# Two of the first loads of a decoder-block kernel move from SyncE's DMA queue to ScalarE's

## The reference

```python
h = rms_norm(x, norm_pre_mix[l])          # x: 512 x 1024
proj = h @ w_in[l]                        # w_in: 1024 x IN_COLS, in tiles of 128 columns
p_rwkv, p_nsa, p_swa, p_gate = _split(proj, (RWKV_COLS, NSA_COLS, SWA_COLS, GATE_COLS))
```

## Time and profile before

| what | us |
|---|---|
| median of 3 runs (lowest, highest) | 971.26 (971.24, 972.1) |
| the profiled execution, its own time | 971.14 |
| span in its trace (first to last instruction) | 969.3 |
| TensorE busy in the span | 949.5 (98%) |
| first matmul with a weight tile starts at | 14.74 |
| x3 issued at; last of it landed after | 2.89; 9.7 |
| w0 issued at; last of it landed after | 2.13; 9.1 |

### The profile page before, as it was taken

How to read it: one execution, slowest core, us unless ns; L and a number is a source line. 1 busy time by engine, 2 the same in 40 slices (tenths; PEclk the granted TensorE clock), 3 DMA queues, 4 the chain that set the end, 5 groups by cost and what they waited for, 6 DMA issues and landing times.

```text
span 969.3 us, 20667 instructions
## 1 busy us (share of the span) xinstructions
PE 949.5 (98%) x8504; PEld 767.3 (79%) x8504; DVE 703.2 (73%) x1170; ACT 422.5 (44%) x846; POOL 439.5 (45%) x473
## 2 busy tenths in 40 slices
PE   7999999999999999999999999999999999999997
PEld 5788777777777777776777888888999888888886
DVE  3799797565655966869777870489787774489987
ACT  4134341323313525546574454553444443345573
POOL 3367547335442865767665466445223225500000
PEclk9999999999999999999999999999999999999999
DMA  9344633212222648525336548043333433345452
GB/s 259 103 131 133 139 87 69 43 35 70 77 59 65 195 131 186 153 67 130 59 100 176 148 150 263 24 152 109 89 111 112 118 96 87 97 142 177 138 194 89
DMA packets 157365, 115.47 MB, mean 119 GB/s; under 512 B 21413, under 2 KB 139951, under 8 KB 157272
## 3 DMA queue, kind: packets, MB, share of 16 engines
q1 hardware_dynamic: 147820, 105.21, 37.8%
q10 hardware_dynamic: 9420, 8.95, 4.0%
q0 software_dynamic: 32, 0.00, 0.0%
HBM read 102.84 MB, written 11.30 MB: 118 GB/s over the span
## 4 chain that ended last, share of the span: by engine, by line
PE 83%; DVE 12%; issue 2%; ACT 1%; DMA 1%; POOL 0%; SPq 0%; DVEq 0%; ACTq 0%
PE ps L2424 32%; PE ps L2903 5%; PE ps L2902 5%; PE ps L2907 5%; PE ps L2544 3%; PE ps L2790 3%; PE ps L2963 2%; PE ps L2964 2%; PE ps L2965 2%; PE ps L2733 2%; PE ps L2940 2%; PE ps L2937 2%; PE ps L2936 2%; DVE XF L1517 2%; PE ps L2438 1%
## 5 line engine op out<-in xcount | busy, mean ns | idle before, releaser
L2424 PE MATMUL ps<-HHI,WHI 128*128 128x512 f32 x440 | 176.8, 402 | 0.7 <-DVE HLO L1549 0.7
L2424 PE MATMUL ps<-HLO,WHI 128*128 128x512 f32 x440 | 176.8, 402 | 0.0
L829 POOL TENSOR_TENSOR WLO<-WRAW,WHI 128x1024 fp32r<-128x1024 f32 (+1 forms) x51 | 103.2, 2026 | 102.1 <-ACT WHI L949 102.0
L930 POOL TENSOR_TENSOR WLO<-WRAW,WHI 128x512 fp32r<-128x512 f32 x50 | 72.5, 1457 | 118.6 <-ACT WHI L1317 117.2
L2424 PE MATMUL ps<-HHI,WLO 128*128 128x512 f32 x440 | 117.6, 397 | 0.0
L870 POOL TENSOR_TENSOR WLO<-WRAW,WHI 128x256 fp32r<-128x256 f32 x136 | 108.7, 802 | 14.4 <-ACT WHI L1166 7.0
L2424 PEld LDWEIGHTS ps<-HHI,WHI 128*128 128x128 f32 x440 | 82.6, 188 | 24.9 <-issue 7.5
L2424 PEld LDWEIGHTS ps<-HLO,WHI 128*128 128x128 f32 x440 | 82.6, 188 | 19.2 <-issue 1.6
L2424 PEld LDWEIGHTS ps<-HHI,WLO 128*128 128x128 f32 x440 | 80.7, 188 | 18.4 <-issue 1.4
L833 POOL CAST WHI<-WRAW 128x256 fp32r<-128x256 f32 (+1 forms) x93 | 46.7, 503 | 100.4 <-PE ps L2424 100.2
L2903 PE MATMUL ps<-HLO,WHI 128*128 128x512 f32 x200 | 77.9, 389 | 0.0
(11 more groups left out here) (512 smaller groups left out, 2316.1 us busy)
## 6 DMA issues: line engine op xcount, KB each, us to landing
WRAW<-in_w_in SPq DMA_DIRECT2D x47, 512.0 KB, 4.5
WRAW<-in_w_gate SPq DMA_DIRECT2D x22, 512.0 KB, 3.8
WRAW<-in_w_up SPq DMA_DIRECT2D x22, 512.0 KB, 3.8
WRAW<-in_w_down SPq DMA_DIRECT2D x19, 512.0 KB, 3.5
spilled<-SQ SPq DMA_DIRECT2D x24, 256.0 KB, 2.5
GATES<-spilled SPq DMA_DIRECT2D x6, 768.0 KB, 5.0
WRAW<-in_w_in SPq DMA_DIRECT2D x16, 256.0 KB, 3.5
WRAW<-in_w_branch SPq DMA_DIRECT2D x32, 128.0 KB, 2.9
```

The source lines that it names most:

```text
L829: return pool.tensor_tensor(lo[:, 0:chunks, :], WRAW[:, n % NRAW, 0:chunks, :], hi[:, 0:chunks, :].bitcast(F32), ALU.subtract)
L930: pool.tensor_tensor(lo, raw_half(item[1], item[2]), hi.bitcast(F32), ALU.subtract).then_inc(w_lo, 1)
L2424: last = pe.matmul(DB[g % 2][:, :], (wlo if which == "low" else whi)[:, c, :], lo if which == "x_low" else hi, start=a == 0, stop=a == 3 * ...
```

## The change

SP no longer issues x1 and w0. ScalarE issues both: x1 between `CONP` and the two `PRAW` loads, and w0 behind the `PRAW` loads, ahead of the square root. On SP's queue x3 moves up right behind x2, and w1 follows it. No semaphore, buffer or computation changes. The queues' orders become:

| queue | before | after |
|---|---|---|
| SP | x0, x1, x2, w0, x3, w1, `HOT`, sinks, `MASK`, w2, ... | x0, x2, x3, w1, `HOT`, sinks, `MASK`, w2, ... |
| ScalarE | `CONP`, `PRAW`, `PRAW` | `CONP`, x1, `PRAW`, `PRAW`, w0 |

```diff
--- before.py
+++ after.py
@@ -725,11 +725,9 @@
             def x_tile(t):
                 sp.dma_start(XTOK0[:, t, :], x[t * P:(t + 1) * P, :]).then_inc(x_in[t], 16)
 
-            for t in range(3):
+            for t in (0, 2, 3):
                 x_tile(t)
             for n in range(FF0):
-                if n == 1:
-                    x_tile(3)
                 if n == 2:
                     sp.dma_start(HOT[:, :], hot).then_inc(hot_in, 16)
                     sp.dma_start(SNK, bass.AP(sinks.tensor, 0, [[0, P], [1, NH]])).then_inc(hot_in, 16)
@@ -763,7 +761,7 @@
                             .then_inc(gates_in[(d - GS) % 2], 16)
                 if n >= NRAW:
                     sp.wait_ge(w_lo, n - NRAW + 1)
-                for part, cols, src in job_sources(n):
+                for part, cols, src in job_sources(n) if n else ():
                     sp.dma_start(raw_of(n)[part, :, cols], src).then_inc(w_loaded[n % NRAW], 16)
             sp.wait_ge(dense_done, OUT0)
             sp.dma_start(XTOK[:, :, :], x.rearrange("(t p) d -> p t d", p=P)).then_inc(xtok_in, 16)
@@ -934,8 +932,11 @@
         def _(act):
 
             act.dma_start(CONP[:, :], con[:, 0:NCONP]).then_inc(con_in, 16)
+            act.dma_start(XTOK0[:, 1, :], x[P:2 * P, :]).then_inc(x_in[1], 16)
             act.dma_start(PRAW[0:NPAR1, 0, :], par1).then_inc(par_in, 16)
             act.dma_start(PRAW[0:NPAR2, 1, :], par2).then_inc(par_in, 16)
+            for part, cols, src in job_sources(0):
+                act.dma_start(raw_of(0)[part, :, cols], src).then_inc(w_loaded[0], 16)
             act.wait_ge(eps_ok, 1)
             act.activation(MISC[:, 70:72], EPSC, ACT.Sqrt)
```

## The result

The changed kernel takes 978.71 us, the median of 4 runs (978.23 to 979.39), against 971.25 (970.96 to 972.1) before. The ratio is 1.0076, with a 95% interval from 1.0058 to 1.0093. It is 7.46 us slower. The forecast was 978.3.

The account below looks back on a forecast made before the run. TensorE, busy 98% of the span, was taken as the bound, so only its start could move: first weight-tile matmul 5.7 us later plus 1.3 us of slow clock, 7.0 us on 971.26, gives 978.3 us; range 971.7 to 981.0.

Parts of the forecast that it names:

- What bounds it: Whole kernel: TensorE is busy 98% of the span, so changed first loads move only the moment at which it gets going.
- Turns packet by packet: First loads: two queues share the DMA engines by packet count, not bytes; 72 packets on q1 against 67 on q10.
- my rival: First loads: queues share in lots of several packets, w0 lands with w1 at 14.4; +2.5 us, 973.8 us; chance 0.10.
- Landings: First loads: x1 and x2 land at about 9.3, x3 at about 10.8, w0 at 17.6 us, between 14.4 and 18.7.
- the few engines: w0's load: on engines holding most `PRAW` packets it waits 41 turns, 1.5 us beside x3 and 2.0 us beside w1.
- the slow partners: End of w0's load: its last 33 packets go beside `HOT`, the sinks and `MASK`, which take 2.6 us.
- From the landing to the first matmul: From w0's landing through `hi_part(0)`, `HHI` and `HLO`: 2.85 us, first weight-tile matmul at 20.45 instead of 14.74 us.
- What was taken as hidden: Start: issues, table load, parameters at about 12 and transposes ending at 15.7 us all come before w0 matters.
- x1's lateness: Start: x1 lands 1.5 us late from taking turns with x2; TensorE still ends its transposes well before w0's part.
- The clock: First matmuls after TensorE's 4.7 us idle: they run slow, costing 1.3 us, between 0 and 2.0.
- The not slower rival: Start: w0 lands by 11.9 us and TensorE's short waits for x go; -0.7 us, 970.6 us; chance 0.10.

Follow-up runs that it names:

- e3: Changed kernel with the 74-row parameter load cut into 64 and 10 rows: 974.17 us, ratio 1.0034 to the kernel before.
- e4: Changed kernel with `HOT`, sinks and `MASK` issued behind w2 instead of ahead of it: 975.08 us, ratio 1.0047 to the kernel before.
- e8: Changed kernel with both the 74-row parameter load cut in two and `HOT`, sinks and `MASK` behind w2: 973.34 us, ratio 1.0022 to the kernel before.
- e1: Half of the change: x1 on ScalarE's queue, w0 back on SP's between x2 and x3: 972.37 us, ratio 1.0013 to the kernel before.
- e6: Changed kernel with w0 ahead of both parameter loads on ScalarE's queue: 979.8 us, ratio 1.0082 to the kernel before.
- e5: Changed kernel with 26 instead of 10 unread transposes ahead of x3's: 978.93 us (975.89 to 981.21), ratio 1.0073 to the kernel before.
- e9: Changed kernel with 26 instead of 10 unread transposes, run again for a second trace: 978.73 us.
- e2: Half of the change: w0 on ScalarE's queue behind the parameters, all four token tiles on SP's: 976.03 us, ratio 1.0049 to the kernel before.

## Why the prediction was right

**What bounds it.** Only the start moved. Of 7.5 us of span, 7.45 stand in the chain before 30.6 us, and no later slack gave any back.

**Turns packet by packet.** That the turn goes by count and not by bytes is shown by 62 against 64 packets of unlike sizes, and by 561 against 560. That it is a single packet is shown by the two series of starts in the section on the result, which also bear out the two engines under a `PRAW` load. The rule of the Trainium skill ("DMA: Bandwidth & Descriptors", "Queues, rings and completion order"), turns in bunches of 9 to 17 descriptors, does not fit them. By my rival w0 would then have landed with w1; w1 landed at 14.1 (2.12 + 12.0), w0 at 17.88.

**Landings.** x1 and x2 were expected at 9.3, x3 at 10.8. TensorE could start on x1 at 8.90, x2 was squared from 8.46 on, and x3 landed at 1.66 + 8.5 = 10.16:

```profile
DMA to landing us min/median/max: 7.2/7.9/8.5
```

(the time to landing of the two token tiles issued from 1.20 and 1.66 us on SP's queue; the largest is x3). All came 0.4 to 0.9 us before the forecast. I had let x2 land no earlier than before, but from 6 to 8 us the engines moved 413 GB/s, with hardly a small packet among them. w0 was expected at 17.6 between 14.4 and 18.7, and landed at 17.88. The two terms under it, the few engines and the slow partners, are shown apart by e3 (2.9 us) and e4 (2.2 us), and together by e8 (3.8 us, for without the first the second has less to act on).

**From the landing to the first matmul.** 2.85 us expected, 2.66 measured (17.88 to 20.54). First matmul 20.45 expected, 20.54 measured.

**What was taken as hidden.** The issues were: ScalarE's five end at 3.42 (w0's took 0.60 us), and the table load runs from 3.45. The parameters came at 12.26 (12 expected), hidden too. The transposes were expected to end at 15.7 and ended at 17.6 (20.54 less the idle of 2.93), since TensorE stayed slow throughout. The hole of 1.39 us for x1 is not enough to explain that: with a hole of 1.42 and 1.43, e3 and e4 had TensorE fast before x3's eleven (1.24 us). Why it stayed slow here is not shown. The forecast was wrong at this point and it did no harm. e1 shows what a slow start is worth once w0 is out of the way: 1.69 us. The forecast called x1's lateness harmless and named no price for it without that cover.

**The clock.** 1.3 us taken between 0 and 2.0; measured 1.65, after an idle of 2.9 us (expected: 4.7). The size of the term came out well with some luck, for the mechanism was partly wrong. I expected the first matmuls to be slow, like the transposes after the idle at the start. They were fast, and the clock fell 0.8 us later. The idle was also shorter than I had it. That idleness brings the fall is likely and not shown: of the traces at the full clock, the three with a fall had 2.50 us of idle or more, but e4 had 2.99 and kept its clock. The page "TensorE: Matmul & The Clock Gate" of the Trainium skill, Part 1, has the clock halved after idleness. The granted clock of 0.50 agrees with the amount and e4 is an idle without it; the full 2.0 us that I drew from the page is above the 1.65 measured.

**The sum.** 5.7 + 1.3 = 7.0 against 5.80 + 1.65 = 7.45. The not slower rival needed w0 by 11.9, and no run with w0 on ScalarE's queue came nearer than 13.6 (e6).

## What to carry to other kernels

A second DMA queue gave a load its turns here, and no bandwidth: beside the other queue every packet waited for one of the other's, so small packets (a weight tile's 512 bytes) lost to big ones. The load that the first useful work needs should not be last on a queue that shares. Look how many DMA engines a small load in front of it uses: here 37 KB in 74 rows, on two engines, made a 512 KB load land 2.9 us later than the same rows cut into 64 and 10. And where a start has several loads that come just in time, ask of each what it costs once the others are early. A loss that was hidden (x1's, 1.25 us in the median when alone) stands beside what is left of the main one when that is mended.

## What the runs showed that I had not expected

Whether the clock falls differs between executions of nearly the same start. An idle of 1.98 (e5), 2.01 (e3) and even 2.99 us (e4) kept it high; idles of 2.50 (e9), 2.93 (the changed kernel) and 3.27 us (e2) did not. The rows of stretches read a granted clock of 1.00 during the slow transposes at the start (6 to 16 us in the changed kernel), though their weight loads take 0.20 us each and not 0.11. That 1.00 is no measurement: the trace's record of the clock has its first entry at 17.95 us in the changed kernel, and at 10.76 us in the kernel before, which is where its weight loads had become fast. At the start one has to go by the length of the weight loads.

ScalarE can be held for long by an issue. With w0 ahead of the parameters, e6, their issues took 2.21 and 3.93 us, and the table load started at 8.38 instead of 3.45. There it was hidden.
